# Folding the sums of later key blocks to 64 rows on VectorE and ScalarE in a stick-breaking attention kernel

## What is computed

```python
P = rmsnorm(x) @ w_in                       # columns of all mixers and gates
# stick-breaking attention, per head
z = q @ k.T / 8                             # q and k RMS-normalised per head
log_beta, log_1m = log_sigmoid(z), where(mask, log_sigmoid(-z), 0)
after = reverse_cumsum_over_keys(log_1m) - log_1m
a = where(mask, exp(log_beta + after), 0)
yc = a @ v
merged = sum_i sigmoid(gate_i) * (branch_i @ w_branch_out[i])
x = x + merged @ w_o
x = x + (silu(g) * u) @ w_down              # g, u = rmsnorm(x) @ w_gate_up
```

## Time and profile before

| | us |
|---|---|
| median of 3 runs | 1675.31 (1673.73 to 1675.38) |
| profiled execution | 1674.12 |
| its span, first to last instruction | 1672.4 |
| TensorE busy (granted clock 0.999) | 1664.4 (100%) |
| VectorE busy | 947.6 (57%) |
| ScalarE busy | 752.5 (45%) |
| GpSimd busy | 180.0 (11%) |

### The profile page before, as it was taken

How to read it: one execution, slowest core, us unless ns; L and a number is a source line. 1 busy time by engine, 2 the same in 40 slices (tenths; PEclk the granted TensorE clock), 3 DMA queues, 4 the chain that set the end, 5 groups by cost and what they waited for, 6 DMA issues and landing times.

```text
span 1672.4 us, 22054 instructions
## 1 busy us (share of the span) xinstructions
PE 1664.4 (100%) x7608; PEld 1386.0 (83%) x7608; DVE 947.6 (57%) x1170; ACT 752.5 (45%) x1059; POOL 180.0 (11%) x171
## 2 busy tenths in 40 slices
PE   9999999999999999999999999999999999999999
PEld 7888888888888888888888888888888888888887
DVE  6887876545454434434649877765555444344344
ACT  7677676333342222223456777763333432232231
POOL 1333311000010000000123242200001100000000
PEclk9999999999999999999999999999999999999999
DMA  5222222333323223223333222223223222233233
GB/s 190 91 75 87 88 85 74 92 97 100 100 95 101 90 99 100 93 96 100 113 127 101 63 88 88 88 70 100 95 92 109 88 101 95 94 100 99 90 100 126
DMA packets 49154, 162.20 MB, mean 97 GB/s; under 512 B 5713, under 2 KB 5969, under 8 KB 49105
## 3 DMA queue, kind: packets, MB, share of 16 engines
q1 hardware_dynamic: 46656, 157.34, 28.8%
q10 hardware_dynamic: 2448, 4.23, 0.7%
HBM read 155.26 MB, written 2.10 MB: 94 GB/s over the span
## 4 chain that ended last, share of the span: by engine, by line
PE 94%; DVE 2%; ACT 1%; DVEq 1%; POOLq 0%; POOL 0%; issue 0%; DMA 0%; ACTq 0%; SPq 0%
PE bank L503 28%; PE bank L504 28%; PE bank L507 28%; PE z L576 2%; PE z L504 1%; PE z L507 1%; PE z L503 1%; PE z L549 1%; PE misc L592 1%; PE misc L590 1%; PE z L550 1%; DVE S L1314 0%; DMA xT<-in_x 0%; DVE N L1195 0%; DVE S L1312 0%
## 5 line engine op out<-in xcount | busy, mean ns | idle before, releaser
L503 PE MATMUL bank<-xg_hi,w_hi 128*128 128x512 f32 x1584 | 621.2, 392 | 0.0
L504 PE MATMUL bank<-xg_lo,w_hi 128*128 128x512 f32 x1584 | 616.8, 389 | 0.0
L816 ACT ACTIVATE w_hi<-raw 128x1024 fp32r<-128x1024 f32 (+1 forms) x294 | 303.5, 1035 | 481.4 <-DMA raw<-in_w_units 480.4
L1183 DVE TENSOR_TENSOR w_lo<-raw,w_hi 128x1024 fp32r<-128x1024 f32 (+1 forms) x294 | 370.1, 1262 | 41.1 <-ACT w_hi L816 22.3
L507 PE MATMUL bank<-xg_hi,w_lo 128*128 128x512 f32 x1584 | 392.1, 389 | 0.0
L507 PEld LDWEIGHTS bank<-xg_hi,w_lo 128*128 128x128 f32 x1584 | 297.3, 188 | 62.2 <-DVE w_lo L1183 0.2
L503 PEld LDWEIGHTS bank<-xg_hi,w_hi 128*128 128x128 f32 x1584 | 297.4, 188 | 61.7 <-issue 0.7
L504 PEld LDWEIGHTS bank<-xg_lo,w_hi 128*128 128x128 f32 x1584 | 297.5, 188 | 61.3 <-issue 0.7
L1188 DVE TENSOR_TENSOR S<-bank,rstd 128x512 f32<-128x512 f32 x152 | 104.9, 690 | 267.3 <-PE bank L507 266.6
L503 PE MATMUL bank<-mid_hi,w_hi 128*128 128x512 f32 x474 | 184.6, 390 | 0.0
L504 PE MATMUL bank<-mid_lo,w_hi 128*128 128x512 f32 x474 | 184.4, 389 | 0.0
(11 more groups left out here) (194 smaller groups left out, 1664.8 us busy)
## 6 DMA issues: line engine op xcount, KB each, us to landing
raw<-in_w_units SPq DMA_DIRECT2D x278, 512.0 KB, 3.3
raw<-in_w_units SPq DMA_DIRECT2D x20, 256.0 KB, 2.9
xT<-in_x SPq DMA_DIRECT2D x8, 256.0 KB, 6.3
mix_hi<-yb_hi ACTq DMA_DIRECT2D x8, 256.0 KB, 2.3
mix_lo<-yb_lo ACTq DMA_DIRECT2D x8, 256.0 KB, 2.4
out_x<-xT SPq DMA_DIRECT2D x7, 256.0 KB, 3.7
ln_g<-in_sgu_ln_g SPq DMA_DIRECT2D x2, 256.0 KB, 4.3
ln_b<-in_sgu_ln_b SPq DMA_DIRECT2D x2, 256.0 KB, 5.0
```

The source lines that it names most:

```text
L503: mm(dst[:, :], wh[:, k0 + k, :], his[k], start=(k % per == 0), stop=False)
L504: mm(dst[:, :], wh[:, k0 + k, :], los[k], start=False, stop=False)
L816: af(w_hi[at.slot(c)][:, 0:kc, :], raw[at.slot(c)][:, 0:kc, :], ACT.Copy).then_inc(hi_done, 1)
L1183: tt(w[:, 0:kc, :], r[:, 0:kc, :], h[:, 0:kc, :].bitcast(F32), ALU.subtract).then_inc(lo_done, 1)
```

## The change

The sums over later blocks are made before TensorE gets them. Per head ScalarE copies the upper 64 rows of blocks 3, 2 and 1 of t_s down to rows 0 to 63 (`fold_halves`), and VectorE adds the lower 64 rows, so that 128 rows become 64, and adds up the blocks (`fold_sums`): `fold12` holds columns for blocks 1 and 2, `fold0` for block 0. ScalarE rounds them (`fold_round`), and VectorE writes the low parts into rows 64 to 127 of the same tiles (`fold_lo`). One pass of `neg_ones` over 128 rows then adds high and low part at once. GpSimd's `suffix` is gone. In the pairs, the squares of q and k go from GpSimd to ScalarE (two squares) and VectorE (the low part). `k_rest` stays on GpSimd, and so do the first squares of each layer.

In the diff, cut to what is spoken of, `tiles` are placed in memory that other tensors don't use at that time.

```diff
@@ gpsimd @@
-            def suffix(h3):
-                pool.wait_ge(sp_ok, h3 + 3)
...
                 with pool.Fori(0, PAIRS - 1) as j:
...
-                    suffix(h3)
-                    head_square(l * 8 + (j * 2 + 3), QT)
-                    head_square(l * 8 + (j * 2 + 4), KT, m + 2)
-                    suffix(h3 + 3)
                     k_rest(l * 8 + (j * 2 + 4))
@@ tensor @@
-            def cumulate(h3, nth):
...
+            def cumulate(h3, nth, tiles):
+                hl0, hl12 = tiles[0], tiles[1]
+                later = {0: hl0[:, :], 1: hl12[:, P:3 * P], 2: hl12[:, 0:P]}
                 pe.wait_ge(sp_lo, h3 + 3)
                 pe.wait_ge(suf_ok, nth + 1)
                 for g, blocks in Z_BLOCKS:
                     for i in blocks:
+                        at, width = Z_AT[i], T - P * i
+                        for s in (s_hi, s_lo):
+                            last = mm(z[g][:, at:at + width], neg_tri[:, :], s[:, S_AT[i]:S_AT[i] + width],
+                                      start=False, stop=(s is s_lo and i == 3), skip_group_check=True)
+                        if i < 3:
+                            last = mm(z[g][:, at + P:at + width], neg_ones[:, :], later[i],
+                                      start=False, stop=True, skip_group_check=True)
                     last.then_inc(cum_done, 1)
@@ scalar @@
+            def fold_halves(tiles):
+                for f, a in ((tiles[3], S_AT[3]), (tiles[2], S_AT[1])):
+                    last = af(f[0:HD, :], t_s[HD:P, a:a + 3 * P], ACT.Copy)
+                last.then_inc(fold_up, 1)
+            def fold_round(nth, tiles):
+                hl0, hl12, f0, f12 = tiles
+                act.wait_ge(fold_sum, nth + 1)
+                act.sem_inc(passed, 1)
+                af(hl12[0:HD, :], f12[0:HD, :], ACT.Copy)
+                af(hl0[0:HD, :], f0[0:HD, :], ACT.Copy).then_inc(fold_hi, 1)
+            def head_square(n_raw, src):
+                act.wait_ge(qk_raw, n_raw)
+                act.sem_inc(passed, 1)
+                af(S2[:, :], src[:, :], ACT.Square)
+                af(sq_hi[:, :], src[:, :], ACT.Square).then_inc(qk_sq_hi, 1)
...
                     softplus_logs(h3)
                     softplus_hi(h3)
+                    fold_halves(folds_last if last else folds)
                     split_hi(at, 3)
...
                     af(v_both[:, :, 0, :], misc[:, :].rearrange("p (n c) -> p n c", c=HD), ACT.Copy).then_inc(v_hi_ok, 1)
+                    fold_round(l * 8 + j * 2, folds_last if last else folds)
+                    if not last:
+                        head_square(l * 8 + (j * 2 + 3), QT)
                     split_hi(at, 5)
                     attention_exp(h3)
...
                     rms_chain(nch, misc, HD, misc_free)
+                    head_square(l * 8 + (j * 2 + 4), KT)
                     split_hi(at, 6)
...
                     split_hi(at, 7)
                     softplus_hi(h3 + 3)
+                    fold_halves(folds)
                     act.wait_ge(misc_done, m0 + 4)
                     act.wait_ge(yc_ok, l * 8 + (j * 2 + 1))
                     rms_chain(nch + 1, misc, HD, misc_free)
                     split_hi(at, 8)
+                    fold_round(l * 8 + (j * 2 + 1), folds)
                     act.wait_ge(qk_nrm, l * 8 + (j * 2 + 4))
                     k_round()
@@ vector @@
+            def fold_sums(nth, tiles):
+                hl0, hl12, f0, f12 = tiles
+                half = slice(0, HD)
+                dve.wait_ge(fold_up, nth + 1)
+                dve.sem_inc(passed, 1)
+                tt(f12[half, :], f12[half, :], t_s[half, S_AT[3]:1280], ALU.add)
+                tt(f0[half, :], f0[half, :], t_s[half, S_AT[1]:S_AT[3]], ALU.add)
+                dve.drain()
+                tt(f12[half, 2 * P:], f12[half, 2 * P:], f12[half, 0:P], ALU.add)
+                dve.drain()
+                tt(f0[half, P:], f0[half, P:], f12[half, P:], ALU.add)
+                dve.drain()
+                dve.sem_inc(fold_sum, 1)
+            def fold_lo(nth, tiles):
+                hl0, hl12, f0, f12 = tiles
+                half, other = slice(0, HD), slice(HD, P)
+                dve.wait_ge(fold_hi, nth + 1)
+                dve.sem_inc(passed, 1)
+                tt(hl12[other, :], f12[half, :], hl12[half, :].bitcast(F32), ALU.subtract)
+                tt(hl0[other, :], f0[half, :], hl0[half, :].bitcast(F32), ALU.subtract)
+                dve.drain()
+                dve.sem_inc(suf_ok, 1)
+            def square_lo(nth):
+                dve.wait_ge(qk_sq_hi, nth + 1)
+                dve.sem_inc(passed, 1)
+                tt(sq_lo[:, :], S2[:, :], sq_hi[:, :].bitcast(F32), ALU.subtract).then_inc(qk_sq, 1)
...
                     softplus_lo(h3)
+                    fold_sums(l * 8 + j * 2, folds_last if last else folds)
...
                     split_lo(at, 3)
+                    fold_lo(l * 8 + j * 2, folds)
                     split_lo(at, 4)
                     v_rest()
+                    square_lo(l * 6 + j * 2)
...
                     head_norm(nch, QT, par[:, R_GQ:R_GQ + 1])
+                    square_lo(l * 6 + (j * 2 + 1))
                     scaled(at, 3, S0[:, :])
...
                     head_norm(nch + 1, KT, par[:, R_GK:R_GK + 1])
                     scaled(at, 5, S2[:, :])
+                    fold_sums(l * 8 + (j * 2 + 1), folds)
                     split_lo(at, 8)
+                    fold_lo(l * 8 + (j * 2 + 1), folds)
                     mixed(m0 + 4, j1)
                     split_lo(at, 9)
```

## The result

The changed kernel takes 1699.01 us (median of 4 runs, 1698.46 to 1700.05), the kernel before beside it 1674.76 (1673.73 to 1675.38). The ratio is 1.0149, 95% interval 1.0136 to 1.0162: slower by 24 us. The forecast was 1697.

A forecast was written before the change was run, and what follows sets the result against it. TensorE, busy 100% at 2.4 GHz, was taken to bound the kernel. Per layer 4.5 + 2 x 3.5 - 0.1 = 11.4 us, +22.8 for two layers on 1674.1, gave 1697 us; range 1680 to 1708.

The forecast's parts named there:

- fold_sums 2.12, fold_lo 1.23: VectorE's two added fold operations: middle-value durations in us, priced by column and instruction with drains.
- The ceiling from q_lo's shifted operations: VectorE's folds: at 0.83 us per piece shifted across partitions, fold_sums at most 2.9 us and fold_lo 1.9.
- Wait ahead of cumulate 1: Head 1 of a non-last pair: folded sums ready 21.5 us after yc_half starts, so TensorE stalls 1.85 us.
- Wait ahead of attend 1: Head 1 of a non-last pair: VectorE needs 9.3 us from cumulate 1, TensorE 7.14, so it stalls 2.15 us.
- q's squares: Head 0 of the next pair: q's square ready at 22.1 us after attention_lo, TensorE there at 21.3; stall 0.8 us.
- The pair: A non-last pair's loop takes 60.2 us against 56.72, +3.5 us, twice per layer (pairs 1 and 2).
- The last pair: Head 0 gains 0.64 us; head 1 stalls 1.2 of the 1.28 gained; net -0.1 us.
- The loop's five terms: Consecutive stretches of one pair's dependency loop: 22.1 + 7.12 + 0.2 + 21.5 + 9.3 = 60.2 us.
- One sign I named: TensorE over the kernel: busy time down by 8 to 10 us while the span grows.
- the covers hold: Attention pairs: added work stays hidden, TensorE gains 10.2 us and the two 0.62 waits: 1662.7 us; chance 0.10.
- The mechanism of k_both beside VectorE: Behind cumulate 1: GpSimd's k_both slows VectorE's split and convolution product by 1.24 us.
- My rival: k_both fully blocks VectorE, 2.5 us instead of 1.24: 1.3 more in 6 pairs, 1705, inside range; no separate chance.

The follow-up runs named there:

- the matmuls alone: The kernel before with cumulate's 11 matmuls and no folds, GpSimd's suffix kept, some needed low parts and later blocks left out: 1666.03 us, ratio 0.9954.
- the squares alone: The kernel before with only the pairs' squares of q and k moved to ScalarE and VectorE, suffix kept on GpSimd: 1672.31 us, ratio 0.9991.
- the folds alone: The changed kernel with the pairs' squares back on GpSimd, the folds kept: 1717.30 us, ratio 1.0262.
- the mixed kernel: The changed kernel with moved folds for head 0 of every pair and the last pair's head 1; other head 1s keep suffix and 16 matmuls: 1668.71 us.
- all folds moved: The changed kernel, same work, with the folds of both heads placed earlier in VectorE's order, in the last pair too: 1682.79 us, ratio 1.0056.
- the shorter fold_sums: The changed kernel whose fold_sums leaves out the two adds across blocks, which the result needs: 1687.70 us.

## Why the prediction was right

By its own steps, first the forecast, then the trace of the changed kernel:

- Cumulate 1.63 us: its first matmul starts at 148.03, its eleventh at 149.59, and with the 0.06 of a 128-column one that is 1.62. Over all heads, the matmuls alone gave 7.8 us where 8.9 were expected.
- fold_sums 2.12, fold_lo 1.23: 1.98, and 1.2 with its signal. A column's price and the fixed part, read from one operation of 512 and one of 1024 columns, held at 384, 256 and 128. The ceiling from q_lo's shifted operations did not: in the kernel before GpSimd's last suffix operation ran beside them (161.18 to 161.92), and without it the same two take 1.39 in place of 1.65 (1.64 in the run with the squares alone, which kept the suffix).
- Wait ahead of cumulate 1: 1.85, measured 1.80 to 1.89. From yc_half (157.88) to fold_lo's end 21.5 were forecast, and 21.6 came (179.44).
- Wait ahead of attend 1: 2.15. The trace names it in three of six pairs only, with 1.6 to 1.7. In the other three TensorE was running at 1.2 GHz and came just in time, so the loss was the same: 9.01 us from cumulate 1 to attend 1, 0.3 less than the 9.3 forecast.
- q's squares: 0.8, measured 0.65 to 0.73; in pair 0 at 90.25, measured 90.17.
- The pair: 60.2, measured 60.38. Attend 1 of pair 0 later by 4.5, measured 4.4 (123.86 to 128.26), or 4.7 counted from the layer's first squares, which come 0.3 earlier in the changed kernel (44.36 and 44.06).
- The last pair: -0.1, measured +0.35 (attend 1 at 293.08 and 305.10, 12.02 later, where pair 2's was 11.67 later). Cumulate's wait was 1.27 for 1.2.
- Sum: 11.4 per layer, measured 12.0 in layer 0 and 12.6 in layer 1 (attend 1 of the last pair at 1123.06 and 1147.67, 24.6 in all).

What was mis-sized is small, and that the pair fits to 0.2 us is in part luck, since errors of up to 0.4 us cancel. The loop's five terms, forecast and measured: the end of attention_lo to q's squares 22.1 and 22.35, the squares to the end of attend 0 7.12 and 7.18, the step to yc_half 0.2 and 0.20, yc_half to cumulate 1 21.5 and 21.73, cumulate 1 to the end of attention_lo 9.3 and 8.88 (attend 1 starts 0.13 behind it). Within the fourth, the stretch up to k's norm took 14.46 for 14.2 and VectorE's part behind it 7.10 for 7.3. I also left out that after a wait the first matmul takes 0.47 to 0.50 us in place of 0.39, so that TensorE is 0.1 us later than the wait alone says.

One sign I named was wrong: TensorE's busy time would fall by 8 to 10 us, and it fell by 0.9. In the stretch from the first squares to the last attend 1 it fell by 0.4:

```profile
44.36:1123.06 1078.70, 1077.44 (x5009) 900.45 (x5008) 666.97 (x830) 551.23 (x816) 161.83 (x146) 1.00 0.28 93
44.06:1147.67 1103.61, 1077.06 (x4930) 893.00 (x4928) 688.47 (x938) 592.47 (x904) 64.73 (x46) 1.00 0.28 90
```

The first row is of the kernel before, the second of the changed one. The matmuls take 10.2 off. The slow stretches put 5.1 back, which are busy time. The rest I estimate from the 19 waits and the rows of TensorE: the last matmul before one counts as busy for 0.16 us longer than its place in a row would take (0.22 for one whose successor starts 0.06 behind it), and the first one after it for 0.1. That is about 0.25 a wait, 4.8 in all against 0.5 for the two waits of before. Together -0.8, near the -0.4 of the rows. For the same reason a list of waits, 26.4 us here, tells less than the loss.

The rivals: "the covers hold" would need nothing to wait, and 26.4 us of waits are there. Its time, 1662.7, is near what I estimate for the matmuls and the squares together, 1674.8 less 7.8 and 1.6 and less the further 1.2 us by which the wait for the squares grew in the run with the matmuls alone: about 1664. No run shows it. The mechanism of k_both beside VectorE was confirmed at 1.12 us for the 1.24 that I took.

The rows show how these 1.12 us come about. k_both is two subtractions. The first takes 1.3 us (from 179.46), and the split that starts within it (180.40) ends at 181.84, about 1.1 behind its end, which is what a split takes alone. The second subtraction takes 2.17, and ends 1.14 behind the split (182.98). The product that starts within that (181.93) ends at 183.52, 0.54 behind. So each engine waited for the other in turn. In the run with the folds alone fold_lo's two subtractions end at 215.23 and 216.76, 0.4 behind GpSimd's sq_hi (214.81) and sq_lo (216.35). The Trainium skill's rule ("SBUF — State Buffer", Who interferes with whom), that of two such instructions the one that comes later is blocked fully, agrees with all of these, taken one instruction at a time. My rival took k_both as a single block, which made it 2.5 us and the time 1705; that reading of the rule is what failed, and not the rule.

## What to carry to other kernels

When the bounding engine is fed by a chain through two others, walk that chain instruction by instruction from the last thing the bound engine gave to the next it wants. Average idle time (12 us of 57 here) says nothing; 4.4 us placed on a chain with 2.6 us to spare, and more behind it, cost over three times what was saved. Keep such work for the places where the walk shows room, as in the mixed kernel, and recount each wait that moves, since an instruction of GpSimd beside it can more than double the price of the step you have just put on the path (fold_lo, 1.03 to 2.8 us).

## What the runs showed of the hardware

TensorE's clock fell to 1.2 GHz behind some waits of about 2 us, and not behind others of the same length. The stretches of the changed kernel around cumulate 1 of pair 0 (start:end, then length, busy time of PE, PEld, DVE, ACT and POOL, granted clock, DMA share, GB/s), in which TensorE had stood for 1.89 us until 119.26:

```profile
118.00:120.00 2.00, 0.74 (x3) 0.66 (x4) 1.66 (x4) 1.97 (x3) 0.89 (x1) 0.94 0.70 205
120.00:122.00 2.00, 2.00 (x11) 2.00 (x9) 1.90 (x3) 1.06 (x3) 1.94 (x2) 0.50 0.14 57
122.00:124.00 2.00, 2.00 (x9) 1.63 (x8) 1.70 (x2) 1.88 (x5) 0.61 (x1) 0.71 0.00 0
124.00:126.00 2.00, 2.00 (x10) 1.66 (x9) 1.59 (x3) 0.12 (x1) 0.00 (x0) 1.00 0.00 0
```

The missing clock adds up to 1.7 us of work (0.06, 0.50 and 0.29 of 2 us each). It happened three times in the changed kernel, behind six waits of 1.8 to 1.9 us ahead of cumulate 1, and not at all in the profiled run with all folds moved, whose six waits were 2.3 to 2.6 us long. Another execution of that same kernel had a mean clock of 0.997 and 1685.15 us, where the profiled one had 1.000 and 1681.73. Both waits of 4.0 and 4.1 us in the run with the folds alone were followed by a fall (0.51 and 0.64 in 90:94, 0.50, 0.50 and 0.81 in 942:948). What a fall costs depends on what TensorE waits for next. In the changed kernel the three cost nothing, since the wait for attend 1 took them in: attend 1 to attend 1 has 60.3 to 60.4 us with and without one. With the shorter fold_sums one fell behind the wait for attend 1 (0.71, 0.50 and 0.94 in 964:970), and the pair has 60.27 us in place of 58.65. So waits of this length cost their own time, 0.1 for the restart, and sometimes up to 1.7 more.
